# Reordering the projection, the paged softmax and the page pairs of a hybrid decoder trunk

## The reference

```python
hc, gc, gb, cq, ckv, kpe = split(a @ w_in)          # 512, 512, 512, 384, 256, 32 columns
y_conv = gb * conv3(gc * hc)                        # returns the last rows of gc * hc too
ckv, kpe = rms(ckv, kv_norm), rope(kpe)
q = rms(cq, q_norm) @ w_uq                          # 8 heads x (64 + 32)
q_lat = einsum('bthn,rhn->bthr', q_nope, w_uk)
# prompt: causal softmax attention over ckv, kpe
# samples: softmax over 16 pages of 128 cached rows and the 4 new rows
past_c, past_p = pool_ckv[page_table], pool_kpe[page_table]
s_past = q_lat . past_c + q_pe . past_p;  s_new = q_lat . ckv + q_pe . kpe
o_lat = softmax([s_past, s_new] * scale) . [past_c, ckv]
y_att = einsum('bthr,rhv->bthv', o_lat, w_uv)
y = concat(y_conv, y_att) @ w_out
```

## Time and profile before

| what | value |
|---|---|
| median of 3 runs | 1529.85 us |
| profiled execution, its own time | 1531.82 us |
| its span, first to last instruction | 1530.0 us |
| mean granted TensorE clock | 0.989 |
| busy: DVE, ACT, POOL | 67%, 18%, 7% |
| chain that ended last: PE, DVE, DMA | 90%, 5%, 2% |
| moved by DMA | 152.36 MB, mean 100 GB/s |

### The profile page before, as it was taken

The page is one execution under the profiler, slowest core; times in us unless marked ns, Lnnn a source line. Parts: engine busy times, 40 slices in busy tenths (PEclk is TensorE's granted clock), DMA queues, the critical chain, the costliest instruction groups (busy, mean ns, idle before and its releaser), DMA issues.

```text
span 1530.0 us, 18923 instructions
## 1 busy us (share of the span) xinstructions
PE 1479.8 (97%) x7084; PEld 1189.5 (78%) x7084; DVE 1018.7 (67%) x2068; ACT 269.4 (18%) x564; POOL 103.0 (7%) x114
## 2 busy tenths in 40 slices
PE   7999989899999999999999899999999999999996
PEld 6887735488888888888877778788888888888885
DVE  3363265868776676766865876877866767767845
ACT  4000034412101001001233321121001011011232
POOL 0002223400000000000200001300000000000100
PEclk9999999999999999999999999999999999999998
DMA  8205677712222222222203211222222222222201
GB/s 320 102 33 165 181 212 211 255 56 83 83 83 83 83 84 83 83 83 97 83 28 142 72 67 55 87 83 81 79 82 79 81 80 80 81 81 95 81 28 59
DMA packets 39470, 152.36 MB, mean 100 GB/s; under 512 B 6674, under 2 KB 19379, under 8 KB 26707
## 3 DMA queue, kind: packets, MB, share of 16 engines
q1 hardware_dynamic: 34258, 134.37, 25.4%
q0 software_dynamic: 5120, 16.78, 3.7%
HBM read 148.11 MB, written 3.02 MB: 99 GB/s over the span
## 4 chain that ended last, share of the span: by engine, by line
PE 90%; DVE 5%; DMA 2%; issue 1%; POOL 1%; SPq 0%; ACT 0%; DVEq 0%; POOLq 0%
PE psum L530 69%; PE psum L500 15%; PE psum L658 1%; DMA arena<-in_keys 1%; DMA ring<-in_weights 1%; PE psum L485 1%; DMA arena<-in_rows,vidx 1%; PE psum L764 1%; POOL arena L434 0%; PE psum L729 0%; PE psum L785 0%; PE psum L826 0%; DVE arena L1151 0%; PE psum L693 0%; PE psum L643 0%
## 5 line engine op out<-in xcount | busy, mean ns | idle before, releaser
L530 PE MATMUL psum<-arena 128*128 128x272 f32 x2016 | 478.9, 393 | 0.0
L530 PEld LDWEIGHTS psum<-arena 128*128 128x128 f32 x2016 | 383.0, 190 | 78.6
L1151 DVE TENSOR_TENSOR arena<-psum,arena 128x272 f32<-128x272 f32 x564 | 249.0, 441 | 248.5 <-PE psum L530 226.1
L530 PE MATMUL psum<-B,ring 128*128 128x272 f32 x736 | 184.7, 393 | 3.2 <-issue 1.8
L500 PE MATMUL psum<-A,ring 128*128 128x272 f32 x704 | 169.8, 403 | 9.0 <-DMA ring<-in_weights 7.8
L500 PEld LDWEIGHTS psum<-A,ring 128*128 128x128 f32 x704 | 136.8, 195 | 40.7 <-issue 11.8
L530 PE MATMUL psum<-arena,ring 128*128 128x272 f32 x672 | 167.7, 392 | 0.0
L530 PEld LDWEIGHTS psum<-B,ring 128*128 128x128 f32 x736 | 139.0, 190 | 32.6 <-issue 2.6
L530 PE MATMUL psum<-A,ring 128*128 128x272 f32 x608 | 152.6, 393 | 1.6 <-DVE A L1594 1.5
L530 PEld LDWEIGHTS psum<-arena,ring 128*128 128x128 f32 x672 | 127.4, 190 | 26.0
L530 PEld LDWEIGHTS psum<-A,ring 128*128 128x128 f32 x608 | 115.4, 190 | 26.0 <-DVE A L1594 2.0
(11 more groups left out here) (224 smaller groups left out, 1250.8 us busy)
## 6 DMA issues: line engine op xcount, KB each, us to landing
ring<-in_weights SPq DMA_DIRECT2D x98, 1024.0 KB, 4.8
arena<-in_keys SPq DMA_DIRECT2D x128, 144.0 KB, 2.9
arena<-in_attw SPq DMA_DIRECT2D x1, 3072.0 KB, 20.9
h<-in_xT SPq DMA_DIRECT2D x4, 544.0 KB, 7.8
out_yT<-A SPq DMA_DIRECT2D x8, 272.0 KB, 2.3
arena<-in_pemb SPq DMA_DIRECT2D x2, 544.0 KB, 5.8
ring<-in_weights SPq DMA_DIRECT2D x2, 512.0 KB, 6.8
arena<-in_bias SPq DMA_DIRECT2D x1, 640.0 KB, 8.5
```

The costliest lines, as they stand in the source:

```text
L530: end = pe.matmul(bank(g, n), lhs[:, c, :], x(c), start=c == 0, stop=c == 3)
L1151: ins = dve.tensor_tensor(out, bank(g, n), more, ALU.add)
```

## The change

- The query-norm tile comes after tile 4 instead of tile 6, then tile 5, the key-norm tile and the queries; tiles 6 to 17 all come after the queries. The tile numbers follow.
- Score pairs 0 to 7 run behind tiles 8 to 15, the new scores of group 0 after them, and tiles 16 and 17 last. ACT makes group 0's exponentials before it waits for tile 17. The convolution's scratch moves to `sq` and `rbuf`, and its two zero columns are set by DVE in each chunk instead of once by POOL. The fourth chunk comes after the key tiles.
- The five turns of group 0 alternate with the key tiles, and values pairs 0 and 1 and score pairs 8 and 9 stand between the value tiles.
- The loop's paged work is four steps earlier; group 1's values pairs are at the steps of `LATE_VALUES`. Gather sets 10 to 13 are released four steps earlier.
- SP issues `keys(2)` ahead of unit 8, and `keys(10)` and `keys(11)` ahead of the stores that wait for the convolution.

```diff
-T_COL = [0, 1, 3, 4, 5, 6, 7, 10, 11, 21, 22, 23, 24, 25, 26, 27, 28, 29]
-T_NQ, T_NKV = 8, 9
-T_UQ = 12
+T_COL = [0, 1, 3, 4, 5, 7, 18, 19, 20, 21, 22, 23, 24, 25, 26, 27, 28, 29]
+T_NQ, T_NKV = 6, 8
+T_UQ = 9
...
+LATE_VALUES = 20, 21, 23, 24, 26, 27, 29, 30
...
-        up = arena[:, 13760:13760 + 1124].rearrange("p (c t) -> p c t", c=2)
+        up = [x[:, :, :].rearrange("p c t -> p (c t)")[:, 0:562] for x in (sq, rbuf)]
...
-            for u in range(4, 9):
+            for u in range(4, 8):
                 unit(u)
-            for m in range(2, 10):
+            keys(2)
+            unit(8)
+            for m in range(3, 10):
                 keys(m)
             sp.wait_ge(dve_x, 4)
             sp.dma_start(a["ckvT"].rearrange("(k p) t -> p k t", p=P), ckv).then_inc(stored, 16)
+            keys(10)
+            keys(11)
             sp.wait_ge(conv_done, 1)
             sp.dma_start(a["kpeT"], ssum[64:96, :]).then_inc(stored, 16)
             sp.dma_start(a["convp"].rearrange("p c t -> p (c t)"), ctails[:, 0:8]).then_inc(stored, 16)
             sp.dma_start(a["convs"].rearrange("p c b t -> p (c b t)"), ctails[:, 8:72]).then_inc(stored, 16)
-            for m in range(10, 16):
+            for m in range(12, 16):
                 keys(m)
...
-            pool.memset(up[:, :, 0:2], 0.0).then_inc(consts, 1)
...
                 if 10 <= s < 14:
-                    pool.wait_ge(sc_full, 2 * s - 3)
+                    pool.wait_ge(sc_full, 2 * s - 7)
...
-            for n in range(2, 7):
+            for n in range(2, 5):
                 in_ab(n)
+            pe.wait_ge(act_x, 3)
+            ones_tile(T_NQ, [qsq[:, i, :] for i in range(3)])
+            in_ab(5)
             pe.wait_ge(act_x, 5)
-            ones_tile(T_NQ, [qsq[:, i, :] for i in range(3)])
             ones_tile(T_NKV, [qsq[:, i, :] for i in range(3, 5)])
-            in_ab(7)
-            in_ab(8)
             pe.wait_ge(attw_loaded, 16)
             pe.wait_ge(dve_x, 3)
             for m in range(8):
...
-            in_ab(9)
-            in_ab(10)
+            in_ab(6)
+            in_ab(7)
             pe.wait_ge(ql_ready, 2)
-            for m in range(7):
-                in_ab(11 + m)
+            for m in range(8):
+                in_ab(8 + m)
                 score_pair(m)
-            score_pair(7)
             score_new(0)
-            for m in range(4):
+            in_ab(16)
+            in_ab(17)
...
+            def up_keys(m):
...
+            def up_values(i):
...
+            turn(0, 0)
+            turn(0, 1)
+            up_keys(0)
+            up_keys(1)
+            turn(0, 2)
+            turn(0, 3)
+            up_keys(2)
+            up_keys(3)
             turn(0, 4)
+            values_pair(0, 0)
+            up_values(0)
+            score_pair(8)
+            up_values(1)
+            values_pair(0, 1)
+            up_values(2)
+            score_pair(9)
+            up_values(3)
 
             def paged(n):
 
-                if n < 16:
+                if n < 12:
                     if n % 2 == 0:
-                        values_pair(0, n // 2)
+                        values_pair(0, 2 + n // 2)
                     else:
-                        score_pair(8 + n // 2)
-                elif n == 16:
+                        score_pair(10 + n // 2)
+                elif n == 12:
                     values_new(0)
                     score_new(1)
-                elif n == 17:
+                elif n == 13:
                     turn_out(0)
-                elif n < 23:
-                    if n == 19:
+                elif n < 19:
+                    if n == 15:
                         pe.wait_ge(ol_ready, 1)
-                    turn(1, n - 18)
-                elif 24 <= n < 32:
-                    values_pair(1, n - 24)
+                    turn(1, n - 14)
+                elif n in LATE_VALUES:
+                    values_pair(1, LATE_VALUES.index(n))
                 elif n == 32:
                     values_new(1)
                 elif n == 33:
...
-                if n < 16 and n % 4 == 3:
-                    raw(1, n // 4)
-                elif n == 16:
+                if n < 12 and n % 4 == 3:
+                    raw(1, n // 4 + 1)
+                elif n == 12:
                     out_scaled(0)
-                elif 17 <= n < 22:
-                    soft(1, n - 17)
+                elif 13 <= n < 18:
+                    soft(1, n - 13)
...
             for r in range(4):
                 raw(0, r)
             act.wait_ge(ql_ready, 2)
+            for n in range(5):
+                soft(0, n)
             act.wait_ge(psum_full, T_COL[17] + 1)
             for hd in range(H):
                 act.activation(K[64:96, hd, :], ssum[64:96, 0:TP], ACT.Copy).then_inc(k_rope, 1)
-            for n in range(5):
-                soft(0, n)
+            raw(1, 0)
...
                 dve.wait_ge(psum_free, T_COL[3 * c + 8] + 1)
-                link(dve.tensor_tensor(up[:, b, 2:UPS], gc[:, 0:TP], hc[:, 0:TP], ALU.mult))
+                link(dve.memset(up[b][:, 0:2], 0.0))
+                link(dve.tensor_tensor(up[b][:, 2:UPS], gc[:, 0:TP], hc[:, 0:TP], ALU.mult))
...
-                if n < 16 and n % 4 == 3:
-                    raw_max(1, n // 4)
-                elif n == 16:
+                if n < 12 and n % 4 == 3:
+                    raw_max(1, n // 4 + 1)
+                elif n == 12:
                     soft_max(1)
-                elif n == 17:
+                elif n == 13:
                     out_turned(0)
-                elif 18 <= n < 23:
-                    if n == 18:
+                elif 14 <= n < 19:
+                    if n == 14:
                         dve.wait_ge(o_full, 1)
-                    turned(1, n - 18)
-                elif n == 23:
+                    turned(1, n - 14)
+                elif n == 19:
...
-            for n in range(6):
-                scaled(n, cq[:, n, :] if n < 3 else ckv[:, n - 3, :] if n < 5 else kx)
-            scaled(6, stg[:, 0, :])
+            for n in range(5):
+                scaled(n, cq[:, n, :] if n < 3 else ckv[:, n - 3, :])
             dve.wait_ge(gains_loaded, 16)
             dve.wait_ge(c_loaded, 64)
             norm_root(1, T_NQ, sq[:, 0, :], QR)
             for i in range(3):
                 link(dve.scalar_tensor_tensor(cq[:, i, :], cq[:, i, :], qgain(i), sq[:, 0, :], ALU.mult, ALU.mult))
             dve.nop().then_inc(dve_x, 3)
+            scaled(5, kx)
             norm_root(2, T_NKV, sq[:, 1, :], R)
             for i in range(2):
                 link(dve.scalar_tensor_tensor(ckv[:, i, :], ckv[:, i, :], kvgain(i), sq[:, 1, :], ALU.mult, ALU.mult))
             dve.nop().then_inc(dve_x, 1)
-            scaled(7, stg[:, 1, :])
-            scaled(8, stg[:, 2, :])
             link(dve.tensor_tensor(rbuf[64:96, 0, :], kx[0:32, :], rope[0:32, 4, :], ALU.mult))
             link(dve.tensor_tensor(rbuf[64:96, 1, :], kx[32:64, :], rope[32:64, 5, :], ALU.mult))
             link(dve.tensor_tensor(ssum[64:96, :], rbuf[64:96, 0, :], rbuf[64:96, 1, :], ALU.add))
...
-            conv(0)
-            for n in range(9, 18):
-                scaled(n, stg[:, (n - 6) % 4, :])
-                if n % 3 == 2:
-                    conv(n // 3 - 2)
-                if n % 2 == 1 and n >= 13:
-                    raw_max(0, (n - 13) // 2)
-            dve.nop().then_inc(conv_done, 1)
-            raw_max(0, 3)
-            soft_max(0)
-            for c in range(4):
+            def keys_up(c):
                 full(T_UK + c)
...
+            for n in range(6, 18):
+                scaled(n, stg[:, (n - 6) % 4, :])
+                if n in (8, 11, 14):
+                    conv(n // 3 - 2)
+                if n in (10, 12, 14):
+                    raw_max(0, (n - 10) // 2)
+                elif n == 15:
+                    raw_max(0, 3)
+                    soft_max(0)
+            turned(0, 0)
+            turned(0, 1)
+            keys_up(0)
+            keys_up(1)
+            turned(0, 2)
+            turned(0, 3)
+            keys_up(2)
+            keys_up(3)
+            turned(0, 4)
+            inverse(0)
+            conv(3)
+            dve.nop().then_inc(conv_done, 1)
             for i in range(4):
-                turned(0, i)
                 full(T_UV + i)
                 dve.tensor_copy(vtok[:, i, :], slot(T_UV + i)[:, 0, :]).then_inc(psum_free, 1)
+                if i == 1:
+                    raw_max(1, 0)
             dve.wait_ge(psum_free, T_OUTAB)
-            turned(0, 4)
-            inverse(0)
```

14 lines of the change are left out of this document (6 added, 8 removed).

## The result

The changed kernel takes **1535.54 us** (median of 22 runs) beside 1530.53 for the kernel before in the same measurement: a ratio of **1.0026, 95% interval [1.0015, 1.0037]**. The same two kernels, measured again in two later batches, gave 1536.75 beside 1530.93 (1.0038 [1.0026, 1.0051]) and 1537.08 beside 1531.19 (1.0036 [1.0022, 1.0049]). So it is slower, by 4 to 6 us. The forecast was 2.2 us faster; the time lies 1.5 us above its range. Disturbed runs are left out of every ratio here.

A forecast was written before the change was run, and what follows sets the result against it. TensorE (PE), busy 97% of the span, bounds the kernel. Loop start 219.7, steps 0 to 11 at 31.1 and the rest at 55.0 end at 305.8 against 308.0: 2.2 us gained, median 1527.7 us, range 1521.5 to 1534.0.

The forecast's parts named there:

- 28.6 - 2.7 = 25.9: Loop from step 24 to the end: 28.6 us before, less 2.7 for the row wait and DVE's pauses, so 25.9.
- DVE's own pauses for PE: Step 24 to the end: DVE's idle pauses while it waits for PE would give 2.1 us.
- 0.6 for the rows: Step 24 to the end: the 2.48 us wait for gathered rows goes, but only 0.6 us of it counts.
- the clock behind the query wait: Query tiles: rival that the clock falls at the new wait, price 4.06 us; 1.9 us lost, 1531.7 us, chance 0.06.
- New wait 2.6: Before the fourth query tile: PE waits 2.6 us for DVE to free a PSUM slot.
- Ahead of the loop: Before the paged loop: waits of 1.7 us at values pair 0 and 1.0 at the value copies, +0.9 net.
- Pair 11: Paged loop: pages land 9.3 us after release, so PE waits 1.0 us; bounds 0 and 3.8.
- Pair 15: Paged loop: PE waits 1.7 us for its pages, as a gather starts 2.5 us after their release.
- The signs of being wrong: Loop start before 217 or after 223, step 12 on under 53 us, or half clock elsewhere than behind the latent queries.
- All page waits go and late values fill gaps: Paged loop: rival that 2.7 us of page waits vanish and late values fill gaps; 6.9 us gained, 1522.9 us, chance 0.30.
- Pages always late: Paged loop: rival that gathers delay the page copies every round and the clock falls; 9.5 us lost, 1539.4 us, chance 0.08.
- Nothing: Paged loop: rival that the gathers' waits move with the pairs and all is as before; 1529.9 us, chance 0.06.

The follow-up runs named there:

- f_rope_pair9_filled: Changed kernel with the key's rope later on DVE, score pair 9 earlier, dummy products ahead of pair 11 and the last two transposes: 1530.38 us, ratio 0.9991.
- g_before_filled: Kernel before the change with eighteen dummy products ahead of page pair 9, nothing moved or held: ratio 1.0005 to the unedited kernel before.

## Why the prediction was wrong

**The step that failed** is "28.6 - 2.7 = 25.9", step 24 to the end, and in it the 2.1 us that "DVE's own pauses for PE" were to give. The stage measured 28.2, 28.3 and 29.1 in the three profiles of the unedited kernel. The other term, 0.6 for the rows, fits: their wait went, and DVE's work in the stage fell by 0.6 (21.38 to 20.79). But DVE's idle time did not shrink. It was 7.2 us of the stage before (28.56 less 21.38) and 7.4, 7.4 and 8.3 after: the 2.1 gave nothing.

The chain that ended last shows what took its place. Before (start, length, what):

```profile
291.65 9.56 DMA arena<-in_rows,vidx
301.22 0.04 issue
301.26 1.07 PE psum L693 x16
```

After, in the same place:

```profile
304.08 0.70 DVE small L1566
...
305.55 0.60 DVE arena L1158
306.15 0.61 DVE arena L1159
...
307.64 0.71 PE psum L796 x4
...
308.38 0.60 ACT arena L1083
...
309.03 1.98 PE psum L808 x16
```

Within the stage, POOL's gathers and their landing make 19.6 us of that chain before, and DVE 0.3. After, DVE makes 17.7 of it (its sums for the output projection among them) and TensorE 8.1 (17.7 and 8.1, 17.7 and 9.2 in the other two profiles). So the gathers had set the end of this stage, and the chain of DVE, ScalarE and TensorE under it was nearly as long: once the rows are in time, it sets the end, at 28. I had seen that DVE keeps its work there and yet took its gaps as room. They are the time in which it waits for TensorE's next block, and taking three values pairs (3.2 us) off TensorE did not close them: TensorE's own waits there rose from 4.3 us, the rows' 2.48 among them, to 5.5 (0.69, 1.18, 0.61, 0.36, 0.58, 1.02, 0.81, 0.26). In the first profile the half clock on the last products is part of this chain too, some 1.2 us (1.98 and 1.45 where the kernel before has 1.09 and 1.12); no run takes it away at no cost, so how the 2.3 divides is not shown.

**The second is the clock behind the query wait.** The wait was forecast to 0.04 us (the sum gave 2.5, "say 2.6", so the last tenth is luck); its after-effect was a rival with a chance of 0.06. Its price was put at 4.06 and is 1.4 (15.42 less 14.02) to 3.1 (17.08 in the second profile). The 2.64 stood open in six profiled executions of the changed kernel and its variants: the five tiles behind it took 15.42, 17.08, 15.70 and 15.71 in four, and 14.02 in two. In the eight where it was 0.4 or filled they took 14.02. It was a likely case, not a rare one. Behind these tiles, the stretch from the latent queries to the first score pair takes 29.3 to 32.3 us in the twelve profiles near 1530 us, at both levels of the clock, whether the query wait was open or not: executions of one kernel differ there by 1.6 us (29.3 to 31.0 for the changed kernel).

The Trainium skill (TensorE: Matmul & The Clock Gate, HAM oscillation) describes an engine that waits for DMAs some 3 to 5 us between bursts and comes back throttled. The forecast called this "just such waits", but 2.64 us is shorter than they are, and here half clock followed it in four executions of six.

Point by point:
- *Queries.* Cover for the scaled queries: right, no wait there. New wait 2.6: 2.64.
- *Ahead of the loop.* 1.7 and 1.0 forecast; 1.91 and 0.85 measured. The loop starts 9.9 us later on average, from the first product, against 8.4 forecast; the clock behind the query wait, 1.5 on average over the three profiles, is about the difference.
- *Pages.* Pair 10 in time: right. Pair 11, forecast 1.0 (bounds 0 and 3.8), waited 2.65, 2.36 and 2.03; in the first of these it also came back at half clock. Pair 15, forecast 1.7: no wait. The gather of set 8 did start beside its copies, 3.0 us after their release (at 247.66, 246.58 and 240.07; forecast 2.5), but the slowest of the copies landed 4.2, 4.6 and 2.3 us after its issue, where it was 6.6 before, and the pair was in time. Steps 0 to 11 came to 31.8 on average against 31.1, and 34.2 in the first profile, where half clock until 237 cost some 3.
- *Steps 12 to 19* 17.8 against 18.3, *20 to 23* 10.1 against 10.8 at full clock, 11.6 where the clock fell.
- *The rows.* The forecast names the late values pair as pair 6, at n = 30; it is the last one, pair 7, at n = 31 (step 31 begins at 297.33). It had no wait, as forecast.
- *The signs of being wrong.* One came true: the clock fell in other stretches than behind the latent queries, at pair 11, in steps 20 to 23 and at the loop's end. Step 12 to the end took 57.6 us in the first profile, over the 53 and over the 55.0 of the forecast too.
- *The rivals.* "All page waits go and late values fill gaps": the waits at 10 and 15 went, the filling gave nothing, as 17.8 and 28.2 show. "Pages always late": no; pairs 12 to 15 never waited. "Nothing": no.

By the terms, in the first pair of profiles: 6.8 us late = start 1.1 + pages and clock 3.1 - 0.5 + 0.8 + end 2.3. In the average of three, on the same reckoning from the first product: start 1.2, loop 3.1.

**What stays open.** The profiles average 1 us apart, the medians 5 to 6. Three and two executions, each some 2 to 3 us off the next and four of the five off their medians towards each other, do not exclude that, but I can't show where the unprofiled runs lose the rest. The account above is thus of the profiled executions: it names what the forecast had wrong, not all that the medians lost. Shown by runs is this much: taking the rope off the path, moving pair 9 and filling the remaining waits brings the changed kernel from 1.0036 to 0.9991 on one chip. The rope has 2.0 (by the ratios) to 2.6 us (by the medians) of this, not clear of noise by itself; how the rest divides between pair 9 and the fills, the profiles don't settle.

## What to carry to other kernels

When work is taken off an engine that waits for another one's chain, ask what the chain's own length is: the wait may simply grow. A wait that goes may have hidden a second chain nearly as long; look for what would end last without it. Treat a new wait on TensorE like those here (2.6 us and more) as one that may have a second price, and look at several profiled executions before calling it none. And before shortening a wait, look at the next one on the same stream (here the last gathered rows): it may take the gain.

## What the runs showed of the hardware

- **Waits, and the clock behind them.** Over the profiles near 1530 us, products came back at 1.2 GHz after waits of 4.80, 5.32, 3.75, 3.38, 2.65 and 2.59 us for pages and 4.78, 3.89 and 2.92 for rows; at 2.4 GHz after 2.48 for rows and 2.36, 2.03, 1.50, 1.13 and less for pages; after the 2.64 for the queries either one. Both levels also came without any long wait: in all five profiles near 1530 us of the changed kernel without the end's dummies, the last 16 products of the loop took 1.97 or 1.98 us instead of 1.09, behind waits of 1.02, 0.81 and 0.26. And behind two waits at the end of step 19, some 0.9 and 0.4 us, the same products came back at 1.2 GHz in three profiles of the changed kernel and its variants and at 2.4 in four.
- **A filled wait is not free.** Two versions with dummies (f_rope_pair9_filled and g_before_filled) had a higher mean clock in their runs than the kernel before beside them (0.9914 and 0.9897, against 0.9871 and 0.9874), and their medians differ from that kernel's by -0.8 and +2.1 us: a float dummy of 256 columns is two records of 0.22 us, and where it stands outside the wait it is pure cost.
- **Chips or sessions differ more than these kernels.** The kernel before had medians of 1530.4 to 1531.2 on four occasions and 1549.6 and 1550.1 on two. On the latter (profiles of the variants only), ScalarE's pauses with the releaser "remote" appear in the loop; they are in none of the twelve profiles near 1530 us.
